# Ten intermediate tensors in HBM are laid out by rows instead of by tiles

## The reference

```
h = modulate(rmsnorm(x), sh1, sc1)
u_a, q, k, v, u_c = split(h @ w_in)
ya = pool_mixer(u_a)              # 256 channels
yb = diff_attention(q, k, v)      # 512 channels
yc = ssm_mixer(u_c)               # 256 channels
ga, gb, gc = split(sigmoid(h @ gate_w + gate_b), 3)
mixed = ga * (ya @ proj_a) + gb * (yb @ proj_b) + gc * (yc @ proj_c)
x = x + g1 * (mixed @ w_out)
x = x + g2 * hier_moe(modulate(rmsnorm(x), sh2, sc2))
```

## Time and profile before

| | |
|---|---|
| time, median of three runs | 2953.89 us |
| the profiled execution's own time | 2954.11 us |
| its span, first to last instruction | 2952.2 us |
| TensorE busy | 2782.0 us, 94% |
| VectorE, ScalarE, GpSimd busy | 1905.2, 1469.0, 369.0 us |
| mean granted TensorE clock | 0.968 of full speed |
| DMA packets, bytes, mean rate | 287584, 554.82 MB, 188 GB/s |
| TensorE busy in 1640 to 1700 us, DMA share there | 60.0 of 60 us, 1.00 |

### The profile page before, as it was taken

One profiled execution on the slowest core, in us unless ns is written; L12 is line 12 of the kernel. 1 busy time (PEld: TensorE's weight loads), 2 busy tenths in 40 slices (PEclk: granted clock), 3 DMA queues, 4 the chain that ended last, 5 costly groups with the idle time before them and its releaser, 6 DMA issues. The chain is left out here.

```text
span 2952.2 us, 41275 instructions
## 1 busy us (share of the span) xinstructions
PE 2782.0 (94%) x13642; PEld 2215.4 (75%) x13643; DVE 1905.2 (65%) x3149; ACT 1469.0 (50%) x2361; POOL 369.0 (13%) x287
## 2 busy tenths in 40 slices
PE   6999998999999988999998999987999999999996
PEld 5768886787877776788876878875777777777774
DVE  6754774746464655644455773457888888888884
ACT  4414664656565553233244342124666666666662
POOL 2101220000000001101010001110222222222211
PEclk8999999999999998999999999998999999999998
DMA  6475324040403137211148995428989989777884
GB/s 234 143 248 193 105 103 164 23 155 31 154 30 129 44 125 237 68 47 50 51 168 295 352 343 204 168 93 301 337 280 298 374 299 304 239 226 228 283 258 134
DMA packets 287584, 554.82 MB, mean 188 GB/s; under 512 B 28748, under 2 KB 95564, under 8 KB 285144
## 3 DMA queue, kind: packets, MB, share of 16 engines
q1 hardware_dynamic: 269048, 492.06, 46.7%
q0 software_dynamic: 14400, 52.44, 7.2%
q10 hardware_dynamic: 4000, 8.53, 0.9%
HBM read 418.21 MB, written 143.15 MB: 190 GB/s over the span
## 5 line engine op out<-in xcount | busy, mean ns | idle before, releaser
L2715 DVE TENSOR_TENSOR moe_w_lo<-moe_W,moe_w_hi 128x1024 fp32r<-128x1024 f32 x384 | 460.4, 1219 | 85.6 <-ACT moe_w_hi L2643 71.7
L2643 ACT CAST moe_w_hi<-moe_W 128x1024 fp32r (+1 forms) x384 | 402.0, 1052 | 148.1 <-PE moe_h1b L2566 76.2
L1631 PE MATMUL project_bank<-h_lo,w_hi 128*128 128x512 f32 x512 | 201.0, 393 | 0.0
L336 PE MATMUL att_bank<-h_hi,w_hi 128*128 128x512 f32 x384 | 168.9, 440 | 13.0 <-ACT att_gates L418 8.1
L2591 PE MATMUL moe_yb<-moe_W,moe_hT 128*128 x384 | 172.5, 592 | 0.0
L427 ACT ACTIVATE att_S<-att_S,att_nm,q_scale 128x128 f32<-128x128 f32 (+15 forms) x128 | 165.7, 1296 | 4.4 <-DVE att_nm L530 4.0
L2564 PE MATMUL moe_h1b<-moe_w_hi,moe_xT_hi 128*128 128x512 f32 x384 | 155.9, 406 | 4.8 <-DVE moe_xT_lo L2726 4.8
L521 DVE TENSOR_SCALAR_CACHE_REDUCE att_S<-att_bank 128x512 f32<-128x512 f32 x192 | 122.3, 687 | 54.8 <-PE att_bank L303 54.8
L338 PE MATMUL att_bank<-h_hi,w_lo 128*128 128x512 f32 x384 | 151.4, 394 | 0.0
L337 PE MATMUL att_bank<-h_lo,w_hi 128*128 128x512 f32 x384 | 151.2, 394 | 0.0
L2566 PE MATMUL moe_h1b<-moe_w_hi,moe_xT_lo 128*128 128x512 f32 x384 | 151.1, 393 | 0.0
(11 more groups left out here) (498 smaller groups left out, 6866.8 us busy)
## 6 DMA issues: line engine op xcount, KB each, us to landing
moe_W<-in_moe_w SPq DMA_DIRECT2D x96, 2048.0 KB, 13.8
w_raw<-in_gate_w SPq DMA_DIRECT2D x48, 512.0 KB, 3.8
out_sg<-gateT SPq DMA_DIRECT2D x32, 768.0 KB, 6.9
gateT<-att_gates SPq DMA_DIRECT2D x48, 256.0 KB, 2.0
gateT<-gate_out SPq DMA_DIRECT2D x48, 256.0 KB, 2.0
early<-in_ada_w SPq DMA_DIRECT2D x8, 1024.0 KB, 12.7
project_spare<-in_x SPq DMA_DIRECT2D x16, 512.0 KB, 6.9
zT<-project_oz SPq DMA_DIRECT2D x32, 256.0 KB, 3.5
```

The source lines that it names most:

```text
L336: pe.matmul(bank[7][:], w_hi[b][:, k, :], h_hi[:, k, at], start=k == 0, stop=False)
L1631: pe.matmul(bank[n % 4][:], w_hi[b][:, k, :], low[:, k, at512(tb)], start=False, stop=False)
L2643: nc.scalar.copy(w_hi[:, slot(p, first), :], raw(at, p)).then_inc(q["w13_high"], 1)
L2715: nc.vector.tensor_tensor(w_lo[:, own, :], raw(at, p), w_hi[:, own, :].bitcast(F32), ALU.subtract).then_inc(q["w1_low" if p < 4 else "w3_l ...
```

## The change

The ten tensors in HBM are redeclared, and every DMA that writes or reads them follows. Nothing changes on the chip's own memories, in the arithmetic or in the waits.

| tensor | before | after | written in pieces of | read in pieces of |
|---|---|---|---|---|
| y_hi, y_lo, mix_hi, mix_lo | [8, 4, 128, 512] | [128, 8, 2048] | 2 KB; attention's y: 2 KB before, 8 KB after | 2 KB |
| qk_hi, qk_lo | [8, 4, 128, 512] | [8, 128, 2048] | 2 KB | 2 KB |
| late_hi, late_lo | [2, 8, 128, 512] | [128, 8, 1024] | 2 KB before, up to 32 KB in a row after | 2 KB |
| gateT | [4, 8, 128, 3, 512] | [24, 128, 2048] | 2 KB | 6 KB before, 2 KB after |

In y and mix, neighbouring partitions of a tile lie 2 KB apart before and 64 KB apart after; in qk 2 KB and 8 KB; in gateT 6 KB and 8 KB; in late (as read) 2 KB and 32 KB. The core of the diff:

```diff
-                        sp.dma_start(to[:, at].bitcast(F32), g[frm][h + first, t]).then_inc(qk_ready[t], 16)
+                        sp.dma_start(to[:, at].bitcast(F32), g[frm][h + first, :, at]).then_inc(qk_ready[t], 16)
...
-                    sp.dma_start(g["gateT"][gu % 2, c % KD, :, c // KD, :], gates[:, gu % 2, :]).then_inc(gate_stored[gu % 2], 16)
+                    sp.dma_start(g["gateT"][c, :, gu % 2 * 512:gu % 2 * 512 + 512], gates[:, gu % 2, :]).then_inc(gate_stored[gu % 2], 16)
...
-                            sp.dma_start(g["y_hi"][h + 2].rearrange("t p n -> p t n"), y_hi.rearrange("p (t n) -> p t n", n=512)).then_inc(q["y_stored"], 16)
+                            sp.dma_start(g["y_hi"][:, h + 2, :], y_hi).then_inc(q["y_stored"], 16)
...
-                sp.dma_start(h_hi[1][:].bitcast(F32), g["late_hi"][1].rearrange("k p n -> p k n")).then_inc(h_ready, 16)
+                sp.dma_start(h_hi[1][:].bitcast(F32), g["late_hi"][:, :, 512:1024]).then_inc(h_ready, 16)
...
-                        for half in range(2):
-                            sp.dma_start(g["late_hi"][half].rearrange("k p n -> p k n"),
-                                         h_hi[1][:, :, half * 512:half * 512 + 512].bitcast(F32)).then_inc(q["kept"], 16)
+                        sp.dma_start(g["late_hi"], h_hi[1][:].bitcast(F32)).then_inc(q["kept"], 16)
...
-            sp.dma_start(y_hi[b][:, k, :].bitcast(F32), hi[k, tb]).then_inc(sem, 16)
+            sp.dma_start(y_hi[b][:, k, :].bitcast(F32), hi[:, k, at512(tb)]).then_inc(sem, 16)
...
-                    sp.dma_start(sg[m % 3][:], g["gateT"][tb, j]).then_inc(g_ready[m % 3], 16)
+                    sp.dma_start(sg[m % 3][:], gateT[:, j, :, at512(tb)]).then_inc(g_ready[m % 3], 16)
...
-                    sp.dma_start(g["mix_hi"][j, tb], mx_hi[:, m % 2, :].bitcast(F32)).then_inc(mix_stored[m % 2], 16)
+                    sp.dma_start(g["mix_hi"][:, j, at512(tb)], mx_hi[:, m % 2, :].bitcast(F32)).then_inc(mix_stored[m % 2], 16)
...
     for n in ("y_hi", "y_lo", "mix_hi", "mix_lo"):
-        g[n] = nc.dram_tensor(n, (KD, TB, P, 512), F32, kind="Internal").ap()
+        g[n] = nc.dram_tensor(n, (P, KD, T), F32, kind="Internal").ap()
...
-    g["gateT"] = nc.dram_tensor("gateT", (TB, KD, P, 3, 512), F32, kind="Internal").ap()
+    g["gateT"] = nc.dram_tensor("gateT", (3 * KD, P, T), F32, kind="Internal").ap()
```

More of the change, by code:

```diff
@@ L269, in _ @@
                             else:
-                                sp.dma_start(late_hi[:].bitcast(F32), g["late_hi"][0].rearrange("k p n -> p k n")).then_inc(q["late"], 16)
-                                sp.dma_start(late_lo[:].bitcast(F32), g["late_lo"][0].rearrange("k p n -> p k n")).then_inc(q["late"], 16)
+                                sp.dma_start(late_hi[:].bitcast(F32), g["late_hi"][:, :, 0:512]).then_inc(q["late"], 16)
+                                sp.dma_start(late_lo[:].bitcast(F32), g["late_lo"][:, :, 0:512]).then_inc(q["late"], 16)
                         if u == NU - 1:
@@ L665, in store @@
         j, half = self.unit(u)
-        c = self.c0 + j
-        sp.dma_start(self.g["gateT"][2 + half, c % KD, :, c // KD, :],
+        at = slice(T // 2 + half * 512, T // 2 + half * 512 + 512)
+        sp.dma_start(self.g["gateT"][bass.ds(self.c0 + j, 1), :, at].rearrange("a p n -> p (a n)"),
                      self.tiles["out"][:, u % 2, :]).then_inc(self.stored[u % 2], 16)
@@ L893, in stage_ssm @@
         ahead.update({n: s.kept_sem(n) for n in ("raw_landed", "y_landed", "sg0_landed", "sg1_landed")})
+        gateT = g["gateT"].rearrange("(b k) p n -> p k b n", b=3)
         with nc.Block() as block:
@@ L923, in load_y @@
                 def load_y(n, k0, k1):
-                    sp.dma_start(ahead[n][:, k0:k1, :].bitcast(F32), g[n][k0:k1, 0].rearrange("k p n -> p k n")).then_inc(ahead["y_landed"], 16)
+                    sp.dma_start(ahead[n][:, k0:k1, :].bitcast(F32), g[n][:, k0:k1, 0:512]).then_inc(ahead["y_landed"], 16)
                 def load_gates(m):
-                    sp.dma_start(ahead[f"sg{m}"][:], g["gateT"][0, m]).then_inc(ahead[f"sg{m}_landed"], 16)
+                    sp.dma_start(ahead[f"sg{m}"][:], gateT[:, m, :, 0:512]).then_inc(ahead[f"sg{m}_landed"], 16)
                 for u in range(32, 38):
@@ L1467, in store_qk @@
                     sp.wait_ge(q["q_split"], m + 1)
-                    sp.dma_start(g["qk_hi"][u, tb], o_hi[:, m % 2, :]).then_inc(qk_stored[m % 2], 16)
-                    sp.dma_start(g["qk_lo"][u, tb], o_lo[:, m % 2, :]).then_inc(qk_stored[m % 2], 16)
+                    sp.dma_start(g["qk_hi"][u, :, at], o_hi[:, m % 2, :]).then_inc(qk_stored[m % 2], 16)
+                    sp.dma_start(g["qk_lo"][u, :, at], o_lo[:, m % 2, :]).then_inc(qk_stored[m % 2], 16)
                 def store_z(n):
@@ L1537, in _ @@
                     if n == 30:
-                        for half in range(2):
-                            sp.dma_start(g["late_hi"][half].rearrange("k p n -> p k n"),
-                                         h_hi[1][:, :, half * 512:half * 512 + 512].bitcast(F32)).then_inc(q["kept"], 16)
-                        for half in range(2):
-                            sp.dma_start(g["late_lo"][half].rearrange("k p n -> p k n"),
-                                         h_lo[1][:, :, half * 512:half * 512 + 512].bitcast(F32)).then_inc(q["kept"], 16)
+                        sp.dma_start(g["late_hi"], h_hi[1][:].bitcast(F32)).then_inc(q["kept"], 16)
+                        sp.dma_start(g["late_lo"], h_lo[1][:].bitcast(F32)).then_inc(q["kept"], 16)
                     if n >= 2 and not is_z[n - 2]:
@@ L1553, in _ @@
                 sp.wait_ge(q["scales"], HEADS * TB)
-                sp.wait_ge(q["kept"], 64)
+                sp.wait_ge(q["kept"], 32)
                 sp.wait_ge(q["later"], 16 * 6)
@@ L2051, in store_mix @@
                     sp.wait_ge(q["mix_split"], m + 1)
-                    sp.dma_start(g["mix_hi"][j, tb], mx_hi[:, m % 2, :].bitcast(F32)).then_inc(mix_stored[m % 2], 16)
-                    sp.dma_start(g["mix_lo"][j, tb], mx_lo[:, m % 2, :].bitcast(F32)).then_inc(mix_stored[m % 2], 16)
+                    sp.dma_start(g["mix_hi"][:, j, at512(tb)], mx_hi[:, m % 2, :].bitcast(F32)).then_inc(mix_stored[m % 2], 16)
+                    sp.dma_start(g["mix_lo"][:, j, at512(tb)], mx_lo[:, m % 2, :].bitcast(F32)).then_inc(mix_stored[m % 2], 16)
                 def load_x(i):
```

22 lines of the change are left out of this document (11 added, 11 removed).

## The result

The changed kernel takes 2995.03 us (median of four runs, 2992.6 to 3001.56) against 2953.94 for the one before: a ratio of 1.0139, 95% interval [1.0127, 1.0152], 41.1 us slower. The profiled execution took 3001.11 us, with a span of 2999.2, 47 us over the span before, so it is one of the slower ones, and what is read from it adds up to some 6 us more than the medians' 41.

What follows compares the result with a forecast made beforehand. PE was taken to bound the merge, the DMA close behind. Terms +0.45 (gate loads), -0.4 (y stores), 0, 0 and +0.1 (issue) summed to +0.15 us; forecast 2954.2 us, range 2951 to 2972.

Steps and rivals of the forecast that it cites:

- What bounds the kernel: Merge: PE is the bound, with units 5.44 us apart and the DMA close behind it.
- Gate loads, packets: Merge: 2 KB instead of 6 KB packets cost +0.15 us a load; +0.45 us reaches PE at block 1.
- Attention's y stores: End of attention: 8 KB pieces land the zero store earlier, -0.4 us (-0.7 to +0.4), all of it showing.
- `late`: Projection stores and pooling loads: 0, with 0.5 us either way kept for the loads.
- Addresses of qk and gateT: Row distance for qk and the gate stores: 0, as off PE's path; zT's store took 2.5 us beside 2.0.
- my cover of 2.8: Merge, block 2: the last y slice lands at 1659.0, 2.8 us before PE wants it at 1661.8.
- Rival A: Merge: y and mix pieces 64 KB apart take more DMA time; 20% more gives 2966.5 us; chance 0.33.
- Rival B: Merge: gate packets alone fill the DMA, +0.25 x 32 = 8 us reaches PE, 2962 us; chance 0.08.
- rival C: Faster: spread addresses or even pieces shorten queues, giving back at most 6 us, 2948; chance 0.05.
- the four cases: Forecast 0.54, rival A 0.33, rival B 0.08, rival C 0.05; stated as faster 0.06, same 0.54, slower 0.40.
- The signs that I named: Merge: a PE wait over 4 us at block 1, or any at block 2, would make the forecast wrong.

Runs made afterwards that it cites:

- e1_qk: Kernel before with only qk_hi and qk_lo laid out by rows 8 KB apart: 2972.3 us, ratio to before 1.0064 [1.0043, 1.0085].
- e2_gate: Kernel before with only gateT laid out by rows 8 KB apart: 2974.67 us, ratio to before 1.0071 [1.0045, 1.0097].
- e6_pad: Changed kernel with rows of qk and gateT lengthened to 10 KB apart: 2950.25 us, ratio to before 0.9997 [0.9983, 1.0012].
- e13_micro2: DMAs only, the kernel's q, k and gate loads in each layout: 16 q and k tiles 13.9 us by tiles, 19.5 at 8 KB, 14.3 at 10 KB.
- e3_ymix: Kernel before with only y and mix laid out by rows, pieces 64 KB apart: 2950.5 us, ratio to before 1.0000 [0.9985, 1.0015].
- e5: Kernel before with each gate load cut from three contiguous tiles, in 2 KB packets: 2953.24 us, ratio to before 1.0010 [0.9992, 1.0028].
- e9: Kernel before with qk by rows and w_raw issued ahead of the sixteen qk loads: 2957.19 us, ratio to before 1.0022 [1.0006, 1.0037].
- e10_micro: DMAs only, twelve stores and loads of 256 KB tiles per row distance: stores 381 to 383 GB/s at eight distances from 2 to 32 KB other than 8.

## Why the prediction was wrong

I forecast 2954.2 us, with 2951 to 2972 as the range; it came to 2995. Step by step:

- **What bounds the kernel: right, and it is what made the loss large.** PE with the DMA close behind it was the right picture of the merge.
- **Gate loads, packets: the size was right, within its bounds.** I took +0.15 us a load with an end at +0.25; 0.24 was measured, and in the kernel it costs 1.0010 [0.9992, 1.0028], nothing to be told. As an estimate from its packet cost, the Trainium skill (DMA: Bandwidth & Descriptors, "Why small descriptors are slow (HBM only)") gives 0.06 us a load; the measured 0.24 is four times that.
- **Attention's y stores: right.** Predicted -0.4 us at the zero store; it lands in 4.7 us instead of 5.2, and PE's idle time behind it is 6.57 us instead of 7.15.
- **`late`: right,** in the time (1.0002) and in the stretch that I named; pooling's wait of 6.04 us went to 4.8, more than my 0.5.
- **Addresses of qk and gateT: this step failed.** I wrote that the zT store "is one sample and 0.5 us later at its worst; as qk and the gate stores are off PE's path, 0 for them". The row was right and was the whole case: 2.5 against 2.0 for the same tile, the only layout of the trace with rows 8 KB apart. Three things went wrong with it. I used it only for the stores, though the same tensors are loaded again, and the gate loads stand in the fullest queue of the kernel. I put it down to one sample, while the page has 32 such stores with a median of 3.5 us. And I never followed the q and k loads to what stands behind them on SP and in the queue, the gate weights. In place of my 0 the runs have +18.9 us for qk (e1_qk) and +20.9 for gateT (e2_gate), and with rows 10 KB apart both are gone (e6_pad).
- **What the gate loads did to PE.** I counted the three loads ahead of the last y slice. The slice itself is late already when it is issued, since SP is held by the issues before it:

```profile
1636.22 0.81 SPq L1997 DMA_DIRECT2D out_y_lo<-y_lo  x1
```

That is 48.5 us after the merge's first gate load (1587.68), where it was 44.6 (1610.43 - 1565.82). It lands 10.8 us later (1647.00), where it took 7.85, and PE is ready for it 0.9 us later than before: 3.9 + 2.9 - 0.9 = 5.9 us, against a wait that grew by 6.0 (8.1 less 2.1). As an estimate from e13_micro2, all seven gate loads that the merge issues ahead of that slice make 7 x 0.9 = 6.3 us. That it comes out so near is in part luck, as the queue isn't full all that time: the DMA share is 0.84 to 0.86 until 1622 us and 0.98 or more only from there on. For block 2, 8 x 0.9 = 7.2 us less my cover of 2.8 would be 4.4; the wait is 2.9. The cover was right in kind. Then the clock, which no step had, adds 9.6 us in the merge to 15.1 us of idle time, and up to 8.9 to 11.4 in attention.
- **Rival A: the right mechanism on the wrong tensors.** It gave distance a price for y and mix, at 64 KB, and took the zT row as evidence against; e3_ymix has 1.0000. With its own 25% on the gate loads, 768 KB at 394 GB/s are 2.0 us and a quarter is 0.5 us, the price would still have been little over half of the 0.9 measured. Its rule from the Trainium skill (DMA: Bandwidth & Descriptors, "Latency and other measured facts"), full rate at 512 KiB and less from 2 MiB on, names no distance below 512 KiB, and its pieces were 16 KiB. Read as "smaller distances are free" it fails here: 64 KB is free, 8 KB is not.
- **Rival B** had too small a price, and **rival C** nothing for it. The chances of faster, same and slower didn't follow from those of the four cases: with a tenth of A under 0.2% they are 0.05, 0.57 and 0.38.
- **The signs that I named did appear.** PE waits 8.1 us at block 1 (I had named 4) and 2.9 at block 2, and from 1664 to 1708 us it is busy for 41.1 of 44 us with 174 matmuls instead of 196. But y and mix are late without having changed in e2_gate, so a late y slice didn't mean rival A.

**Shown and argued.** Shown: rows 8 KB apart in qk and gateT cause the loss (e1, e2, e6), neither 64 KB nor the packets do (e3, e5), and in attention the greater part passes through the late `w_raw` (e9: two thirds by the medians, 12.6 of 16.3 us by the traces). A pad also moves the tensors to other addresses; that it is the distance is shown by e10_micro and e13_micro2, where other tensors at other addresses are slow at 8 KB and not at 10. Argued from traces only: that the clock's part would go with the waits (both did in e6_pad), and that in e2_gate it is the gate loads that cost, and not the gate stores, which changed with them. Open: why 8 KB is bad when 10 and 64 KB are not, which no run here can see; why single-stream loads at 4, 16 and 32 KB lie in between, and whether other patterns would be hurt there.

## What to carry to other kernels

When a layout changes, count the bytes between neighbouring partitions of a tile, and look in the trace for a transfer that already has that distance: compare its time by itself with one of the same size in contiguous memory, and if it is slower by a quarter, apply that to every load and store of the changed tensors. Then follow each slower load to the small load behind it in the same queue and to whoever waits for that one. Padding the rows is a cheap test: here 2 KB at the end of a row took a 41 us loss away, and made the kernel before 0.2% faster when applied to a tensor that it had all along.

## What the runs showed of the hardware

- 2 KB pieces in rows exactly 8 KB apart are slow: 16 tiles of 256 KB load in 19.5 us instead of 13.9, 215 instead of 302 GB/s. In the middle of such a stream (412 to 427 us of e13_micro2) it is 252 GB/s at a DMA share of 0.95, by tiles (384 to 394) 372 at 1.04: most of the loss is packets that take longer. Stores go at 359 instead of 381 GB/s. Rows 10 KB apart need 14.3, and stores 64 KB apart are at 381.
- Three pieces of 2 KB, 256 KB apart, instead of one of 6 KB cost a 768 KB load 0.24 us in a stream of eight.
- An idle time of 8.1 us in the middle of a stretch of matmuls was followed by 5.7 us at half the clock (0.43 us a matmul instead of 0.23). Over the merge all slower stretches together were 9.6 us beside 15.1 of waiting. After a wait of 3.1 us in attention the clock stayed at 1.00.
